# Router scores with tokens on partitions: hT's tiles as the stationary piece, eight products for each tile

## The reference

```python
def route(hf, w_router, b_router):
    T = hf.shape[0]
    scores = jax.nn.sigmoid((hf @ w_router).astype(jnp.float32))      # (1024, 16)
    sel = scores + b_router.astype(jnp.float32)
    sel_g = sel.reshape(T, N_GROUPS, EXPERTS_PER_GROUP)
    group_score = jnp.sum(lax.top_k(sel_g, TOP_K)[0], axis=-1)
    g = jnp.argmax(group_score, axis=-1)
    in_group = jnp.take_along_axis(sel_g, g[:, None, None], axis=1)[:, 0]
    _, local = lax.top_k(in_group, TOP_K)
    idx = g[:, None] * EXPERTS_PER_GROUP + local
    w = jnp.take_along_axis(scores, idx, axis=1)
    return idx.astype(jnp.int32), w / jnp.sum(w, axis=-1, keepdims=True)

# in each layer
x = x + g1 * mixer(modulate(rms_norm(x, norm1_g[layer]), sh1, sc1))
h = modulate(rms_norm(x, norm2_g[layer]), sh2, sc2)
x = x + g2 * moe_ffn(h, w_router, b_router, ...)   # route, then two experts for each token
```

## Time and profile before

| | us |
|---|---|
| three runs, median (lowest, highest) | 2038.99 (2036.3, 2039.76) |
| the profiled execution | 2046.61 |
| its span | 2044.8 |
| PE busy | 1905.0, 93% |
| DVE busy | 1183.9, 58% |
| ACT busy | 481.6, 24% |
| POOL busy | 300.8, 15% |

### The profile page before, as it was taken

The page is one execution under the profiler, slowest core; times in us unless marked ns, Lnnn a source line. Parts: engine busy times, 40 slices in busy tenths (PEclk is TensorE's granted clock), DMA queues, the critical chain, the costliest instruction groups (busy, mean ns, idle before and its releaser), DMA issues.

```text
span 2044.8 us, 50163 instructions
## 1 busy us (share of the span) xinstructions
PE 1905.0 (93%) x19832; PEld 1150.0 (56%) x19832; DVE 1183.9 (58%) x2132; ACT 481.6 (24%) x1016; POOL 300.8 (15%) x460
## 2 busy tenths in 40 slices
PE   6999999999999978999999699999899589999993
PEld 3444444445666645777777487655445456666661
DVE  3547600368889964333334589999995433333336
ACT  3101000356777840000000140000535000000002
POOL 0001030000000012222222310000001122222233
PEclk8999999799999988999999899999999699999997
DMA  9557520100440088777985913033106899874457
GB/s 395 228 206 281 213 63 0 42 11 11 165 165 11 12 324 314 290 276 255 352 327 202 361 43 109 21 107 107 50 0 235 285 405 407 307 270 175 174 179 265
DMA packets 122589, 390.93 MB, mean 191 GB/s; under 512 B 23776, under 2 KB 44896, under 8 KB 118240
## 3 DMA queue, kind: packets, MB, share of 16 engines
q1 hardware_dynamic: 72720, 303.48, 38.9%
q0 software_dynamic: 21712, 66.46, 9.1%
q10 hardware_dynamic: 28032, 19.17, 3.1%
HBM read 336.80 MB, written 47.49 MB: 188 GB/s over the span
## 4 chain that ended last, share of the span: by engine, by line
PE 76%; DVE 17%; DMA 4%; issue 1%; ACT 1%; SPq 1%; ACTq 0%; POOL 0%; DVEq 0%; POOLq 0%
PE ps L1732 24%; PE ps L1742 12%; DVE kv L1438 11%; PE ps L1558 10%; PE ps L1669 5%; PE ps L1613 5%; PE ps L1627 4%; PE ps L1863 4%; PE ps L1640 4%; PE ps L1652 4%; DMA kv<-in_w_ada 2%; PE ps L1777 1%; PE ps L1535 1%; DMA kv<-in_w_gate_up 1%; DVE pbuf L1085 1%
## 5 line engine op out<-in xcount | busy, mean ns | idle before, releaser
L1732 PE MATMUL ps<-kv,hT 128*32 128x256 f32 x5504 | 387.7, 381 | 5.3 <-DMA kv<-in_w_gate_up 5.3
L1732 PEld LDWEIGHTS ps<-kv,hT 128*32 128x32 f32 x5504 | 226.9, 110 | 82.1 <-issue 8.0
L1438 DVE SCALAR_TENSOR_TENSOR kv<-kv,cols 128x640 f32<-128x640 f32 (+1 forms) x330 | 265.0, 803 | 11.1
L1295 DVE TENSOR_TENSOR hT<-hT,modc 128x256 f32<-128x256 f32 x146 | 62.1, 425 | 302.9 <-PE ps L1732 302.8
L1558 PE MATMUL ps<-hT,ring 128*128 128x512 f32 x512 | 224.3, 599 | 1.2 <-DVE hT L1065 1.2
L805 ACT ACTIVATE hT<-ps 128x128 f32<-128x128 f32 x146 | 40.6, 278 | 747.8 <-PE ps L1732 747.8
L1791 PE MATMUL ps<-hT,ring 128*128 128x320 f32 (+1 forms) x704 | 205.7, 452 | 0.0
L1098 DVE TENSOR_TENSOR_SCAN pbuf<-hT 128x128 f32<-128x128 f32 (+7 forms) x128 | 173.2, 1353 | 47.3 <-ACT hT L747 46.9
L1791 PEld LDWEIGHTS ps<-hT,ring 128*128 128x128 f32 x704 | 132.7, 190 | 69.1 <-issue 2.4
L1558 PEld LDWEIGHTS ps<-hT,ring 128*128 128x128 f32 x512 | 97.6, 192 | 125.8 <-issue 123.9
L1732 PE MATMUL ps<-ring,hT 128*32 128x256 f32 x2560 | 150.8, 388 | 13.0 <-DVE hT L1295 11.4
(11 more groups left out here) (284 smaller groups left out, 2412.3 us busy)
## 6 DMA issues: line engine op xcount, KB each, us to landing
kv<-in_w_gate_up SPq DMA_DIRECT2D x136, 512.0 KB
kv<-in_w_ada SPq DMA_DIRECT2D x20, 2048.0 KB, 7.8
ring<-in_w_gate_up SPq DMA_DIRECT2D x80, 512.0 KB
kv<-in_w_down SPq DMA_DIRECT2D x48, 512.0 KB
ring<-in_w_down SPq DMA_DIRECT2D x40, 512.0 KB
hT<-in_w_gate_up SPq DMA_DIRECT2D x40, 512.0 KB
expert_rows<-hT ACTq DMA_DIRECT2D x584, 32.0 KB
ring<-in_w_in SPq DMA_DIRECT2D x32, 512.0 KB, 6.2
```

Source lines behind the costliest of these rows:

```text
L1438: ins = V.scalar_tensor_tensor(new, old, w_dw_c[:, c, k:k + 1], new, ALU.mult, ALU.add)
L1732: ins = mm(bank(0)[UNIT * q:UNIT * (q + 1), 0:2 * P], xT[:, c, :], wset[s][q // 2][:, 512 * c + 256 * (q % 2):512 * c + 256 * (q % 2) + 25 ...
```

## The change

It swaps the two sides of the router's products. A tile of hT, 128 features by 128 tokens, is the stationary piece, and 16 columns of wr move; the output has tokens on partitions, 16 columns for each of the eight tiles, all in one bank. The products of a tile are made as soon as it is evicted, between the turns of the next ones. One sigmoid over all eight tiles follows, into SBUF, and sets score_done itself. The transposes of the scores, the tile scT and its semaphores, and VectorE's copy are gone. The sigmoid's table is brought in by a one-column activation after the last eviction, in both layers. The last turn of norm 1 uses bank 2 in place of bank 4, so it no longer waits for tile 5's eviction.

```diff
@@ turn_bank, logits_bank
             if n == 1:
-                return 4 * (t % 2)
+                return 2 if t == TT - 1 else 4 * (t % 2)
...
-        def logits_bank(l, half):
-            return 4 + half if l else 7 - half
+        def logits_bank(l):
+            return 4 if l else 7
+
+        scores = spare[:, 0:TT * E]
@@ ScalarE
-            def keep_scores(l, half):
-
-                act.wait_ge(logits_done[l], half + 1)
-                nc.scalar.activation(scT[:, half, :], bank(logits_bank(l, half))[:, 0:P], ACT.Sigmoid).then_inc(scT_made[l], 1)
+            def keep_scores(l):
+
+                act.wait_ge(logits_done[l], TT)
+                nc.scalar.activation(scores, bank(logits_bank(l))[:, 0:TT * E], ACT.Sigmoid).then_inc(score_done[l], 1)
...
             def moe(l):
-                keep_scores(l, 1)
+                nc.scalar.activation(table_ahead[:, 2 + l:3 + l], eps[:, :], ACT.Sigmoid)
+                keep_scores(l)
...
-            norm_keep(1, 4)
-            nc.scalar.activation(table_ahead[:, 3:4], eps[:, :], ACT.Sigmoid)
-            norm_keep(1, 5)
-            norm_keep(1, 6)
-            keep_scores(0, 0)
-            norm_keep(1, 7)
+            for t in range(4, TT):
+                norm_keep(1, t)
             moe(0)
...
             norm_keep(3, 5)
-            keep_scores(1, 0)
             norm_keep(3, 6)
@@ VectorE
-                sc, sel, rank, best = (tmp(n) for n in range(4))
+                sel, rank, best = (tmp(n) for n in range(1, 4))
+                sc = scores.rearrange("p (t e) -> p t e", t=TT)
...
-                score = bank(6)[:, 0:TT * 32].rearrange("p (t e) -> p t e", t=TT)[:, :, 0:E]
-                biased = mark(V.tensor_tensor(sel, score, brt[:, :].unsqueeze(1).to_broadcast([P, TT, E]), ALU.add))
-                V.tensor_copy(sc, score)
-                after(biased)
+                step(V.tensor_tensor(sel, sc, brt[:, :].unsqueeze(1).to_broadcast([P, TT, E]), ALU.add))
@@ TensorE
-            def logits(n, half):
-                tiles = range(TT // 2 * half, TT // 2 * (half + 1))
-                for t in tiles:
-                    turned(n, t)
+            def logits(n, t):
+                turned(n, t)
                 for c in range(DC):
-                    for g, t in enumerate(tiles):
-                        ins = mm(bank(logits_bank(n // 2, half))[32 * g:32 * g + 32, 0:P], wr[:, c, :], hT[:, c, t * P:(t + 1) * P],
-                                 start=(c == 0), stop=(c == DC - 1), skip_group_check=True)
+                    ins = mm(bank(logits_bank(n // 2))[:, E * t:E * (t + 1)], hT[:, c, t * P:(t + 1) * P], wr[:, c, 0:E],
+                             start=(c == 0), stop=(c == DC - 1), skip_group_check=True)
                 ins.then_inc(logits_done[n // 2], 1)
...
             def moe(l):
-                pe.wait_ge(scT_made[l], 2)
-                for half in range(2):
-                    ins = nc.tensor.transpose(bank(6)[:, P * half:P * half + P], scT[:, half, :], ident[:, :])
-                ins.then_inc(score_done[l], 1)
-
                 pe.wait_ge(picked[l], 1)
...
             turn(1, 4)
             turn(1, 5)
-            logits(1, 0)
+            for t in range(4):
+                logits(1, t)
             turn(1, 6)
+            logits(1, 4)
             turn(1, 7)
-            logits(1, 1)
+            for t in range(5, TT):
+                logits(1, t)
             moe(0)
...
             turn(3, 5)
-            logits(3, 0)
+            turned(3, 3)
+            for t in range(5):
+                logits(3, t)
             turn(3, 6)
+            logits(3, 5)
             turn(3, 7)
-            logits(3, 1)
+            for t in range(6, TT):
+                logits(3, t)
             moe(1)
```

More of the change, by code:

```diff
@@ L150, in trunk @@
         y_new = kv[:, o_:o_ + D]
-        scT = oT[:, 0:2, :]
         hflat = hT[:, :, :].rearrange("p c t -> p (c t)")
@@ L222, in trunk @@
         both = lambda name: [sem(f"{name}{l}") for l in range(2)]
-        scT_made = both("scT_made")
         logits_done, score_done, picked, counted, hot_made = (
```

## The result

The changed kernel takes 2065.71 us (median of 4 runs, 2064.31 to 2068.84), the kernel before 2038.52 (4 runs, 2036.3 to 2039.76). The ratio is 1.0137, 95% interval 1.0122 to 1.0152: 27.2 us slower, where 28.2 had been forecast (2067). The profiled execution took 2064.31 us, its span 2062.5.

The account below looks back on a forecast made before the run. It took the serial chain through both routers as the bound, TensorE carrying 76% of the last-ending chain. Streams +14.95 and +15.0, less 1.78 behind them, gave +28.2 us on 2038.99: 2067 us, range 2052 to 2076 (0.8).

Parts of the forecast that it names:

- Pitch: New router products on TensorE: each 128 x 128 load sets the spacing, 107 ns at full clock, 214 at half.
- rival (a): Clock stays at 2.4 GHz in both router streams, 15.6 us each: +4.6 us, 2043.6; chance 0.11.
- The clock falls in a stream that is never idle: Both routers' streams of 144 slots fall to half clock though TensorE's queue is full; chance 0.76.
- D: Time from a router stream's start until the clock falls: taken as 3.6 us; 2 to 6 gives +31.4 to +23.4.
- s + 30.8 - D + 0.2: End of a router's product stream begun at s, drain included: 769.45 and 1605.8 us, +14.95 and +15.0.
- The tail: From the router's last product to routing's second VectorE step: 0.71 us after the change, 1.60 before.
- -0.89 us: Gain behind each router's products, with two transposes (0.70) and VectorE's copy (0.20) gone; -1.78 for both.
- What was priced at nothing: In the routers, the new bank's removed wait and the 1.28 us table load beneath the last products: worth nothing.
- Downstream: Behind the routers, gather, weight loads and DMA stall shift with routing; first unit's clock effect, up to 3 us, taken as 0.
- (b): Clock falls in one router's stream and not the other, or later: +16.4 us, 2055; chance 0.06.
- (c): Router loads pipeline like narrower ones, pitch below 91 ns; at 30 ns -10.2 us, 2029; chance 0.04.
- (d): Nothing moves, since something beside the router's chain (h's stores, POOL's gather) holds routing back: 2039; chance 0.03.

Follow-up runs that it names:

- e2: Changed kernel with 128 moving columns in each router product in place of 16: 2058.46 us, ratio 1.0023 to the kernel before.
- e3: Changed kernel with every tile's eight router products made twice: 2134.66 us in one run, beside 2053.45 for the kernel before.
- e6: Changed kernel, unchanged, profiled again on the chip of e5: 2064.55 us, ratio 1.0133 to the kernel before.
- e4: Kernel before (old products, transposes, copy) with only bank 2, the late sigmoid table and no sigmoid between evictions: ratio 0.9965 to before.
- e5: Kernel before, unchanged, profiled again on the same chip as e6: 2036.58 us in one run.
- e9: e4 plus unread dense products before the second half of the router's products, three in layer 0, two in layer 1: ratio 0.9975 to before.
- e12: e9 again, on the chip of e11: ratio 0.9971 to the kernel before.
- e11: e4 again, on the chip of e12: ratio 0.9979 to the kernel before.

## Why the prediction was right, point by point

**Pitch.** 107 and 214 ns from L1526's rows. Right. A tile's 16 instructions take 3.43 us with about 0.2 to drain, so 0.21 us a slot at half clock. At full clock the 3.20 us from 1588.20 on hold 30 loads, 107 ns each. With 128 moving columns e2 shows 111 ns ((7.31 - 0.3)/63), so its stream takes 16.2 us, not the 15.6 of rival (a).

**The clock falls in a stream that is never idle.** Right in all six streams with 16 columns that were profiled (two each in the first profile, e3 and e6); e2 shows that the few moving columns are the cause, and that the clock is most of the price. The rows of before did not show this much: in the earlier trace rows such work did not lift the clock from 0.50, and that it would also lose a clock of 1.00 was an analogy. The 115 matmuls of the last of these rows had 128 or 256 moving columns, so that row says only that a full queue is not enough; why the clock stayed at 0.50 there no run shows. Rival (a) doesn't fit, for TensorE had no gap and lost the clock. The Trainium skill (TensorE: Matmul & The Clock Gate, Why this matters for your kernels) advises to leave TensorE no idle gaps between bursts of matmuls; by these streams that is not enough.

**When it falls.** D = 3.6 us was taken. By s + 30.8 - D + 0.2 the streams of 26.3 and 27.4 us give D of 4.7 and 3.6, those of e6 (25.6 and 27.6) 5.4 and 3.4. So the term was 0.5 us too short on average in the first profile and 0.8 in e6; over two routers the first is the 1.0 us by which 28.2 exceeds 27.2. The bounds of 2 to 6 hold all four. D had been read from falls behind pauses in which TensorE mostly stood idle, another case than a stream without a pause, so that it fits this closely is partly luck; why it differs by up to 2 us between streams stays open.

**The tail.** 0.71 us from the last product to the second step of routing; measured 767.26 - 766.59 = 0.67. Right, and with it nearly the -0.89 us: the sum took L1180's start from the chain (756.10), by the timeline it is 756.02, which makes it -0.85. L1170 takes 0.29 us from SBUF, as L1174 did from PSUM.

**What was priced at nothing.** The wait of turn(1, 7) and the table load: in the changed kernel ACT's load ran at 758.09, under the last products, and cost nothing. Right there; in e4, with the old products, the same parts are worth 1.9 to 2.0 us a router, where 1.6 had been worked out: the clock, back at 1.00 for the two transposes, adds the rest.

**Downstream.** Shift without gain or loss: right by e5 and e6. SP's load of expert 1 was issued at 756.57, 16.3 us after the first product, where 759, 17 us after it, had been worked out, and hid. The one row that misled was TensorE's 5.3 us wait for weights, which belongs to that execution more than to the kernel: 1.6 in e5.

**Rivals.** (b), (c) and (d) did not occur. (c) needed a pitch under 91 ns. Against (d) the steps of the chain were said to follow within 0.1 us; one wait is 0.24, at 750.62 ahead of L1549, which changes nothing.

## What to carry to other kernels

Which side of a small product is stationary decides its price: a 128 x 128 f32 piece costs its load, 107 ns an instruction at 2.4 GHz, however few columns move, and 128 columns under it cost hardly more (111). With 16 columns such a stream also loses the clock while TensorE is never idle in the records, here some 3 to 5.5 us behind its start, so price it at half clock from there on, and look for a row of the same kind (many loads, hardly a moving column) before trusting a busy share. When a profile of before lies off its median, take a second one before reading a difference of stages into the change.

## What the runs showed of the hardware

More columns made the program faster: with 128 in place of 16 moving columns under the same 128 loads of a router, the granted clock stayed at 1.00, each stream took 16.2 or 16.3 us in place of 26.3 or 27.4, and the time fell by some 22 us (e2). Two products of 384 columns (1.46 us) in layer 1 and three (2.10 us) in layer 0, in gaps in which the clock had mostly fallen, kept it at 1.00 for the second half (3.61 to 1.95 us, e9 and e12). And in layer 1 a gather that started 1.5 us sooner after the first router product slowed down from 2.80 to 4.19 us (e11, e12), since it then met the end of transfers that it had run behind before.
